# A PSUM bank asked for block by block, and new tiles for the squares of d_k, in a four-layer fp32 kernel on one core

## The reference, cut to what matters

```
# a layer of the second kind (two of them; the first kind has other branches, the same frame)
z = rms(x, norm_mix_g) @ w_in                       # split into the columns below
h   = mlstm(conv(m_q), conv(m_k), m_v, gates)       # 4 heads of 128
y_a = sigmoid(m_o) * rms(h, m_norm_g)
sq  = rope(rms(s_q)); sk, sv = from rms(s_ckv)      # 8 heads of 64; sk is normed and turned too
y_b = sparse_attention(sq, sk, sv, top 64 of an index score)
dq  = rope(rms(d_q)); dk = rope(rms(d_k))           # 4 x 2 heads of 64
y_c = rms(diff_attention(dq, dk, d_v, lam))
merged = g0 * (y_a @ w0) + g1 * (y_b @ w1) + g2 * (y_c @ w2)
x = x + merged @ w_out
x = x + (silu(rms(x) @ w_gate) * (rms(x) @ w_up)) @ w_down
```

## Time and profile before

| | |
|---|---|
| median of 3 runs | 1842.03 us (1839.53 to 1842.12) |
| the profiled execution | 1840.88 us, its span 1839.2 us, 36333 instructions |
| PE, PEld busy | 1781.1 us (97%), 1734.7 us (94%) |
| DVE, ACT, POOL busy | 1360.9 us (74%), 1072.6 us (58%), 190.8 us (10%) |
| mean granted clock of TensorE | 0.997 |

### The profile page before, as it was taken

One profiled execution on the slowest core, in us unless ns is written; L12 is line 12 of the kernel. 1 busy time (PEld: TensorE's weight loads), 2 busy tenths in 40 slices (PEclk: granted clock), 3 DMA queues, 4 the chain that ended last, 5 costly groups with the idle time before them and its releaser, 6 DMA issues.

```text
span 1839.2 us, 36333 instructions
## 1 busy us (share of the span) xinstructions
PE 1781.1 (97%) x14784; PEld 1734.7 (94%) x14784; DVE 1360.9 (74%) x2385; ACT 1072.6 (58%) x1808; POOL 190.8 (10%) x200
## 2 busy tenths in 40 slices
PE   8999999999999999999999999999999998999998
PEld 8999999999999989999999888999999988899998
DVE  6998789867899779876768867655557687676553
ACT  5455656654454657654775675544458757755442
POOL 1012410001002410001201003000002100030000
PEclk9999999999999999999999999999999999999999
DMA  8545536564645536664646634555555564355553
GB/s 284 178 151 186 191 122 202 194 206 134 204 161 184 184 127 206 195 205 140 192 147 170 202 103 141 177 198 194 194 156 180 160 195 132 106 169 194 196 194 104
DMA packets 90342, 320.08 MB, mean 174 GB/s; under 512 B 10528, under 2 KB 12992, under 8 KB 90048
## 3 DMA queue, kind: packets, MB, share of 16 engines
q1 hardware_dynamic: 90176, 317.75, 52.5%
HBM read 310.60 MB, written 1.08 MB: 169 GB/s over the span
## 4 chain that ended last, share of the span: by engine, by line
PE 73%; DVE 15%; ACT 6%; issue 4%; POOL 1%; DMA 1%; SPq 0%; DVEq 0%; ACTq 0%; POOLq 0%
PE big L588 67%; PE small L588 4%; DVE POOL L1467 4%; DVE L L1110 4%; ACT H L1886 2%; PE small L587 1%; DVE POOL L1299 1%; DVE POOL L1665 1%; ACT POOL L2270 1%; POOL POOL L2482 1%; ACT POOL L2308 1%; ACT L1982 0%; DVE gates L1354 0%; POOL POOL L2461 0%; DVE FL L1277 0%
## 5 line engine op out<-in xcount | busy, mean ns | idle before, releaser
L588 PE MATMUL big<-HH,H 128*128 128x256 f32 x3344 | 941.5, 282 | 9.6 <-DVE gates L1354 4.8
L588 PE MATMUL big<-HL,H 128*128 128x256 f32 x3344 | 927.4, 277 | 3.9 <-DVE HL L1245 3.8
L588 PE MATMUL big<-HH,L 128*128 128x256 f32 x3344 | 926.2, 277 | 0.0
L1110 DVE TENSOR_TENSOR L<-F,H 128x1024 fp32r<-128x1024 f32 x574 | 703.7, 1234 | 205.6 <-ACT H L1886 204.3
L1886 ACT ACTIVATE H<-F 128x1024 fp32r<-128x1024 f32 x582 | 610.7, 1055 | 205.7 <-PE big L588 202.2
L588 PEld LDWEIGHTS big<-HH,H 128*128 128x128 f32 x3344 | 630.1, 188 | 14.6 <-issue 5.9
L588 PEld LDWEIGHTS big<-HL,H 128*128 128x128 f32 x3344 | 630.3, 188 | 7.8 <-DVE HL L1245 5.9
L588 PEld LDWEIGHTS big<-HH,L 128*128 128x128 f32 x3344 | 629.9, 188 | 0.0
L588 PE MATMUL big<-FH,H 128*128 128x256 f32 x848 | 238.5, 281 | 0.0
L588 PE MATMUL big<-FH,L 128*128 128x256 f32 x848 | 234.4, 276 | 0.0
L588 PE MATMUL big<-FL,H 128*128 128x256 f32 x848 | 234.3, 276 | 0.0
(11 more groups left out here) (237 smaller groups left out, 1795.4 us busy)
## 6 DMA issues: line engine op xcount, KB each, us to landing
F<-in_stream SPq DMA_DIRECT2D x582, 512.0 KB, 4.1
POOL<-POOL SPq DMA_DIRECT2D x32, 128.0 KB, 4.0
POOL<-head_rows SPq DMA_DIRECT2D x8, 256.0 KB, 5.2
X<-in_x SPq DMA_DIRECT2D x2, 512.0 KB, 4.4
POOL<-POOL SPq DMA_DIRECT2D x16, 64.0 KB, 3.1
out_x<-X SPq DMA_DIRECT2D x1, 1024.0 KB, 3.9
POOL<-in_decay SPq DMA_DIRECT2D x1, 768.0 KB, 11.6
POOL<-POOL SPq DMA_DIRECT2D x8, 96.0 KB, 5.2
```

The lines of the kernel that those rows point to most:

```text
L588: return pe.e.matmul(out_, lhsT, rhs, start=start, stop=stop)
L1110: v.tensor_tensor(L[:, j % NR, :], F[:, j % NF, :], H[:, j % NR, :].bitcast(F32), ALU.subtract).then_inc(s_lo, 1)
```

## The change

Two things. First, in channel_blocks the bank of member i is asked for just ahead of block i, for the first n blocks, and no longer ahead of block 0 for all n members. Second, the squares of d_k go to tiles 41-44. ACT's wait ahead of d_k 0 is then for the mLSTM's last gated head instead of for the keys of s_k, and the sparse task's copy into SPT waits until PE has read the squares of d_k, instead of for the mLSTM.

```diff
-        SQ, SK, SV, DQ, DK, DV_, HSQ = 33, 37, 29, 8, 12, 59, 45
+        SQ, SK, SV, DQ, DK, DV_ = 33, 37, 29, 8, 12, 59
+        HSQ = {"s_q": 45, "s_k": 49, "d_q": 45, "d_k": 41}
...
             def channel_blocks(g):
 
                 n = len(g.members)
-                banks_ = [bank_for(m) for m in g.members]
+                banks_ = []
                 for i in range(g.nblocks):
                     if i == middle(g):
                         yield
+                    if i < n:
+                        banks_.append(bank_for(g.members[i]))
...
-                    sq = tile(HSQ + 4 * (n % 2) + i)
+                    sq = tile(HSQ[name] + i)
...
                         act.wait_ge(idx_v.sem, idx_v.at(m.l, 1, "acc", 1, 1))
-                        act.wait_ge(rp_v["s_k"].sem, rp_v["s_k"].at(m.l, "key"))
-                with_squares(m, tile(TURNED[m.label][0] + m.j), tile(HSQ + 4 * (n % 2) + m.j),
+                        act.wait_ge(ml_g.sem, ml_g.at(m.l, "y", 3))
+                with_squares(m, tile(TURNED[m.label][0] + m.j), tile(HSQ[m.label] + m.j),
...
-                    act.wait_ge(ml_g.sem, ml_g.at(l, "y", 3))
+                    is_filled("hd_q", l, "d_k")
                     bank, read = is_filled("st", l, t, u)
```

## The result

The changed kernel's median is 1836.03 us (1832.14 to 1838.52, 9 runs), that of the kernel before on the same chip 1841.88 us (1837.81 to 1844.37, 9 runs). The ratio is 0.9968, with an interval of 0.9957 to 0.998: 5.9 us less, between 3.7 and 7.9. The prediction was 1836.5 us, and faster.

A forecast was written before the change was run, and what follows sets the result against it. PE, busy 97% of the span, was taken as the bound, so only its idle time could be won. 2.8 plus 2.1 us off 1840.88 gave 1836.0, set at 1836.5 for the median; range 1833.0 to 1840.2.

The forecast's parts named there:

- The two places: Where PE would start earlier: out in all four layers, d_v in the third and fourth.
- the sum: Gains at out (2.8 us) and d_v (2.1 us) add to 4.9 us; chance 0.57.
- d_v: Third and fourth layers: starts 1.04 us earlier each, then held by the L part behind the key multiply; 2.1 us together.
- All of it reaches the end: Behind d_v's start, PE and DVE pass on all 1.04 us per layer.
- The cover of 0.53 us: DVE's slack ahead of the L part of piece 334: 1021.95 against DVE free at 1021.42.
- out: Once a layer, PE's second round of blocks comes 0.70 us earlier; four times, 2.8 us.
- has to wait for 217.61 as all three had to before: First layer: out 2 still starts at 217.61, 0.21 us after the multiply of y2 6 ends.
- 0.43 for out 2's first block: First layer: that block, behind a wait, runs from 217.61 to 218.04, when the second round begins.
- Most woven groups gain nothing: The bank edit gains nothing at groups behind a norm or at down 0 and 1; only out is left.
- The added waits cost nothing: ACT's wait for y 3 ahead of d_k 0 and the copy into SPT's wait for PE: cost 0 each.
- Rivals (1) to (3): In order: only out gains, 1838.6 us, chance 0.12; more than the sum, 1833.4, 0.08; nothing at all, 1841.4, 0.07.
- Rival (4), the clock: Behind norms, one clock fall more or less, 1.64 us: 1838.1 or 1834.9, chance 0.10; slower end 1846.3, 0.05.

The follow-up runs named there:

- banks_asked_last: The kernel before, with the waits for the L part and for x moved ahead of out's three bank waits: 1840.93 us.
- key_wait_kept: The changed kernel with ACT's old wait for the keys of s_k put back beside the new one ahead of d_k 0: 1839.74 us.
- low_ahead_of_key: The changed kernel, with DVE making the L part of d_v's first piece ahead of the key multiply: 1834.15 us.
- bank_alone: The kernel before with only the bank edit, each member's bank asked for just ahead of its first block: 1838.22 us against 1841.35, ratio 0.9984.
- squares_alone: The kernel before with only the squares of d_k moved to tiles 41-44 and their waits changed: 1839.56 us against 1841.35, ratio 0.9995.
- changed_fourth: The changed kernel unaltered, run again in a later set: 1835.77 us (12 runs) against the kernel before at 1839.65, ratio 0.9973.
- changed_third: The changed kernel unaltered, run again in another set: 1834.48 us (11 runs) against the kernel before at 1840.31, ratio 0.9967.
- changed_again: The changed kernel unaltered, its first rerun: 1834.87 us (6 runs) against the kernel before at 1844.2, ratio 0.9954.
- both_ahead: Changed kernel; DVE makes the L part of d_v's first piece before the key multiply, and y2's gate multiply before the HL part: 1833.0 us and 1832.96.
- three_ahead: both_ahead with y2's gate multiply moved ahead of the L part too: 1835.29 us (12 runs) against the kernel before at 1840.31, ratio 0.9967.

## Why the prediction was right

**The two places and the sum.** Both edits act where they were costed, by the mechanism given, and each alone gives its own part. The sum was 2.8 + 2.1 = 4.9; the steps measure 3.3 + 2.2 = 5.5, the medians 5.9 (3.7 to 7.9).

**d_v: right.** Predicted 1.04 us each, measured 1.10 and 1.10. The L part behind the key multiply is the next bound, as said, and the wait for it is 0.65 us where about 0.7 was said. The small rest is that the matmul follows the L part by 0.15 us, not by the 0.21 that I took over from the gate multiply. key_wait_kept shows that the wait alone held it.

**All of it reaches the end: right.** From d_k 3 to y2 7 it was 1139.00 - 1009.07 = 129.93 us and is 128.88: 1.05 of 1.10 in the third layer; in the fourth 130.14 and 129.04, all 1.10. The missing 0.05 goes with VectorE's wait of 0.07 us for the spread rows of d_k in the profile after (1034.99 to 1035.06): in traces without that wait it is 129.86 to 129.96 with the old wait (before, banks_asked_last, key_wait_kept) and 128.74 and 128.76 without. The cover of 0.53 us held, and 0.47 were measured. Its limit is seen in low_ahead_of_key, where of the next 0.81 us a part is lost.

**out: right in mechanism, too small in size.** Predicted 4 x 0.70, measured 0.83, 0.82, 0.80 and 0.86. The mis-sized term is the start of out 2, "has to wait for 217.61 as all three had to before": this kept the 0.21 us from the multiply's end to the matmul, and it is 0.05 with one bank wait ahead of one block instead of three ahead of a group. That is 0.16 us more, less 0.03 for the longer block: 0.70 + 0.13 = 0.83. 0.43 for out 2's first block was about right too (218.74 - 218.28 = 0.46). "Most woven groups gain nothing" holds: of TensorE's other waits in the big banks none moved by more than 0.2 us.

**The added waits cost nothing: right.** ScalarE's row for L2002 has TensorE alone as releaser.

**Rivals (1) to (3)** fall by bank_alone and squares_alone: the d_v part is not taken back, nothing beyond the two places came, and the gains pass the norms. Laid beside each other matmul by matmul from 184 us on, the kernel before and the changed one part by more than 0.15 us, and stay apart, at six starts (four of out, two of d_v), at the two falls of the clock and at the wait of 500 us, and nowhere else.

**Rival (4), the clock.** It is real as a size, 1.64 us for a fall behind a norm, and it isn't the change's. The kernel before ran 11 times in one set with times from 1839.67 us (mean clock 0.999) to 1845.6 us (0.995). The changed kernel shows no fall in the first two layers in its first trace, one in changed_fourth (behind 240 us) and two in changed_third (behind 240 and 440 us). In changed_again, whose profiled execution took 1841.2 us, TensorE first stood 4.18 us at 503 us for VectorE, and a fall came behind that (0.83 over 500 to 520 us); the stretch is 6.0 us longer than in the profile after, and falls behind 680 and 860 us cost 1.6 each. Why VectorE came so late there is open. The falls behind 240, 440, 680 and 860 us come and go with and without the change, and cost 1.6 to 1.7 us in each of the traces that have one.

A line through the 171 runs with a clock on record, with one slope, one level for the kernel before and one for every other kernel in each set, gives 1.55 us for each 0.001 of mean clock and leaves a scatter of 1.5 us. At equal clock the changed kernel lies 5.3, 4.3, 4.6 and 5.7 us under the kernel before in its four sets (each ±0.9 to 1.3), both_ahead 8.5 and 8.1, bank_alone 4.3 (±1.0) and squares_alone 1.3 (±0.9). The last two sum to 5.6 as the steps do (3.3 + 2.2), but each lies at the edge of its own step. The line is rough: some falls lower the mean clock and cost nothing, as the last section shows. The Trainium skill (TensorE: Matmul & The Clock Gate, Part 1: The HAM clock gate) says that the gate's timing runs free of a kernel's start; that the falls differ between runs of one kernel agrees with it.

## What to carry to other kernels

A wait list tells what an engine waited for, not what it will win: look which value it needs next and when that one is made. Of ScalarE's 8.0 us 1.1 came through, because VectorE's L part comes 0.8 us after TensorE is ready for d_v; of TensorE's 4.8 us 3.3, because the last of three banks kept its time. Ask for a resource just ahead of its own use; the last one to come free then sets the time, and reading the others earlier is worth nothing (three_ahead). And when two profiles differ by more than the medians, take out of both the falls of the clock, and the waits elsewhere that scatter, before you give the rest to the change.

## What the runs showed that I had not expected

The time from the end of a VectorE instruction to the matmul that it releases isn't one number. For the same multiply it was 0.21 us with three bank waits and two further, satisfied waits in TensorE's program, 0.15 with these two moved ahead, and 0.05 with one bank wait just ahead of its block. 0.06 of it is shown to lie with the waits behind; the other 0.10 is not explained.

A fall of the granted clock has no fixed price. Behind 240, 440, 680 and 860 us, where TensorE then runs a stream without waits, one cost 1.6 to 1.7 us. Behind 1060 us (third layer) and 1540 us (fourth), where TensorE has small steps between its streams, it cost nothing. The profile of before has the one at 1060 us (0.91 over 1060 to 1080 us), that of after doesn't. Before and then after, a matmul ahead of the fall, and the small matmuls that wait for VectorE behind it:

```profile
1058.02 0.28 PE L588 MATMUL big<-HH,H 128*128 128x256 f32 x1
...
1073.02 1.13 PE L588 MATMUL small<-POOL 128*128 128x512 f32 x2 [0.27 <-DVE FL L1709]
```

```profile
1052.32 0.28 PE L589 MATMUL big<-HH,H 128*128 128x256 f32 x1
...
1067.34 1.13 PE L589 MATMUL small<-POOL 128*128 128x512 f32 x2 [1.71 <-DVE FL L1712]
```

Between the two rows lie 15.0 us with the fall and without it, and 15.01 to 15.03 in all fourteen traces: the 1.6 us that the slower matmuls cost are taken from a wait that was there anyway. Around 1540 us the traces with a fall and without one agree within 0.1 us over 39 us as well.
